# Recurrent core of a hybrid decoder step: the sample tile's heads stacked two to a quad slot, one on each half of the partitions

## The reference, cut to what matters

```
def step(S, inp):
    r_t, k_t, v_t, kk_t, a_t, w_t = inp
    sa = jnp.einsum('bhij,bhj->bhi', S, -kk_t)
    S = S * w_t[:, :, None, :] + sa[..., None] * (kk_t * a_t)[:, :, None, :] + v_t[..., None] * k_t[:, :, None, :]
    return S, jnp.einsum('bhij,bhj->bhi', S, r_t)
S_T, y = lax.scan(step, wkv0.astype(jnp.float32), seq)
```

## Time and profile before

| what | us |
| --- | --- |
| timed runs, median (lowest to highest) | 2816.4 (2814.28 to 2817.8) |
| profiled execution, its own time | 2817.6 |
| its span, first to last instruction | 2815.9 |
| recurrent core, first turn to last state product | 966.6 to about 1380 |
| quads 0 and 1 (samples, first half of the heads) | 966.56 to 1029.15 |
| quads 6 and 7 (samples, second half, with eight prompt steps) | 1159.23 to 1232.02 |

### The profile page before, as it was taken

One profiled execution on the slowest core, in us unless ns is written; L12 is line 12 of the kernel. 1 busy time (PEld: TensorE's weight loads), 2 busy tenths in 40 slices (PEclk: granted clock), 3 DMA queues, 4 the chain that ended last, 5 costly groups with the idle time before them and its releaser, 6 DMA issues. The chain is left out here.

```text
span 2815.9 us, 34250 instructions
## 1 busy us (share of the span) xinstructions
PE 2583.5 (92%) x13680; PEld 1442.8 (51%) x13680; DVE 748.5 (27%) x1366; ACT 454.5 (16%) x899; POOL 177.2 (6%) x180
## 2 busy tenths in 40 slices
PE   7999998999988888988699797799999999999996
PEld 4656765555554766766544555444333433443332
DVE  1045702122113635545420211211111121111112
ACT  2121023333323312112100212000000000000001
POOL 0000003011010122223000000000000000000000
PEclk9999999999998869779799986899999999999998
DMA  5512353777762101000244215399999999999996
GB/s 176 165 60 90 120 163 110 273 247 272 266 222 76 64 8 24 1 16 14 106 155 149 91 60 190 135 420 407 392 406 404 391 405 405 403 393 389 405 420 243
DMA packets 198788, 615.14 MB, mean 218 GB/s; under 512 B 37566, under 2 KB 113149, under 8 KB 147501
## 3 DMA queue, kind: packets, MB, share of 16 engines
q1 hardware_dynamic: 186045, 572.78, 53.2%
q0 software_dynamic: 10272, 35.96, 3.9%
q10 hardware_dynamic: 2320, 4.23, 0.4%
HBM read 600.66 MB, written 15.01 MB: 219 GB/s over the span
## 5 line engine op out<-in xcount | busy, mean ns | idle before, releaser
L360 PE MATMUL bank<-ht,w 128*128 128x320 f32 (+1 forms) x1888 | 566.3, 441 | 3.7 <-PEq L237 2.6
L2481 PE MATMUL bank<-wexp,fr 128*64 128x512 f32 x2048 | 445.7, 593 | 1.5 <-DVE fr L2392 1.5
L360 PEld LDWEIGHTS bank<-ht,w 128*128 128x128 f32 (+1 forms) x1888 | 342.0, 192 | 140.5 <-issue 29.5
L2481 PEld LDWEIGHTS bank<-wexp,fr 128*64 128x64 f32 x2048 | 149.1, 137 | 282.8 <-issue 281.5
L2534 PE MATMUL bank<-wexp,ut 128*64 128x512 f32 x1024 | 223.5, 594 | 11.4 <-ACT ut L2444 11.0
L2399 DVE TENSOR_TENSOR x<-x,bank 128x512 f32<-128x512 f32 x160 | 110.0, 688 | 376.4 <-PE bank L2493 368.4
L2534 PEld LDWEIGHTS bank<-wexp,ut 128*64 128x64 f32 x1024 | 72.0, 137 | 152.5 <-issue 136.5
L2461 PE MATMUL bank<-oh,hn 128*128 128x256 f32 x512 | 129.4, 396 | 8.2 <-DVE oh L2385 6.8
L1082 PE MATMUL bank<-work,fr 128*128 128x512 f32 x256 | 116.4, 614 | 6.7 <-DMA work<-in_w_out 5.7
L2493 PE MATMUL bank<-ys,sg 128*128 128x512 f32 x256 | 115.8, 606 | 2.0 <-ACT sg L2434 2.0
L2461 PEld LDWEIGHTS bank<-oh,hn 128*128 128x128 f32 x512 | 93.1, 192 | 46.3 <-issue 27.3
(11 more groups left out here) (403 smaller groups left out, 2686.7 us busy)
## 6 DMA issues: line engine op xcount, KB each, us to landing
wexp<-in_w_e SPq DMA_DIRECT2D x384, 1024.0 KB, 12.2
w<-in_w_in SPq DMA_DIRECT2D x29, 2048.0 KB, 8.6
work<-in_cache_k SPq DMA_DIRECT2D x64, 512.0 KB, 5.4
x<-in_cache_v POOLq DMA_DIRECT2D x64, 512.0 KB, 5.7
work<-in_w_out SPq DMA_DIRECT2D x4, 2048.0 KB, 19.1
work<-in_w_out SPq DMA_DIRECT2D x2, 4096.0 KB, 13.2
work<-in_w_cq SPq DMA_DIRECT2D x1, 4096.0 KB, 13.8
ckk<-in_cache_mem_k SPq DMA_DIRECT2D x8, 512.0 KB, 7.7
```

Source lines behind the costliest of these rows:

```text
L360: ins = e.matmul(self.bank[self.bank_no[n]][:width, 0:TOK], self.w[:, c % 2, k, j:j + width], self.ht[:, k, :], start=(k == 0), stop=(k == ...
L2481: ins = e.matmul(half(bank[u // 4], a_), xg[buf][:, kk, P * h + SLOTS * a_:P * h + SLOTS * a_ + SLOTS], w[:, u % RING, a_, DE * k:DE * k + ...
```

## The change

For the sample tile the two quads of a group become one quad of eight heads. What was a head's slot now holds a pair of heads: the 64 tokens of one on partitions 0 to 63, those of the other on partitions 64 to 127. Each matmul of a slot becomes two, one with its operands and its output on the lower half, one on the upper (`each`, and the loops over `r`). The instructions of DVE, ACT and POOL then take 128 partitions where they took 64, once where they came twice. The eight turns of a quad become 32 matmuls of 64x64 by a 64-wide part of the identity. POOL's spread is written as eight instructions of 512 elements in place of twice four of 1024. A spot of a merged quad holds two of the 16 places, so that group 3 has one prompt step at every spot where it had one at every second. Maps and additions go through their banks in two turns (b = 0, 1), and the second waits for the copies of the first. The masks `ab8`, `lo8` and `em8` are repeated on the upper half. Prompt quads keep their instructions; only the numbers that they wait for are counted anew (`f0`).

```diff
-    em8 = p[:, None] // CS == np.arange(8)[None, :]
+    em8 = p[:, None] % SS // CS == np.arange(8)[None, :]
...
+    tms, bxs, vxs = view(wf, 10240, 4, 4, HD), view(xf, 0, 4, 8, HD), view(xf, 2048, 4, 8, HD)
...
     def quads():
+        k = 0
         for gi, (hg, ti) in enumerate(GROUPS):
             t0, m = TILES[ti]
-            for q in range(2):
-                yield 2 * gi + q, gi, hg, ti, t0, m, q, 4 * hg + 2 * q
+            for q in range(1 if ti == 2 else 2):
+                yield k, 2 * gi + q, gi, hg, ti, t0, m, q, 4 * hg + 2 * q
+                k += 1
+
+    def taken(buf, f, ti, i):
+        return buf[:, f // 2 % 2, 2 * (f % 2) + i, :, :]
+
+    def places(ti, q, spot):
+        return (2 * spot, 2 * spot + 1) if ti == 2 else (8 * q + spot,)
...
-            for k, gi, hg, ti, t0, m, q, hp in quads():
-                em = cw("em16" if ti < 2 else "em8")[:m, 0:E].unsqueeze(2)
+            for k, f0, gi, hg, ti, t0, m, q, hp in quads():
                 g.wait_ge(tm_read, 2 * k + 2)
                 if k:
-                    g.wait_ge(add_made, k)
+                    g.wait_ge(add_made, f0)
+                if ti == 2:
+                    em = cw("em8").unsqueeze(2).to_broadcast([P, 8, HD])
+                    for dst, col in ((bxs, 1), (vxs, 3)):
+                        for v_ in range(4):
+                            ins = g.tensor_tensor(dst[:, v_, :, :], tms[:, v_, col, :].unsqueeze(1).to_broadcast([P, 8, HD]), em, ALU.mult)
+                            if v_ % 2:
+                                ins.then_inc(bv_spread, 1)
+                    send(gi, range(16))
+                    continue
+                em = cw("em16").unsqueeze(2).to_broadcast([P, E, P])
                 for dst, col in ((bx, 1), (vx, 3)):
                     for p_ in range(2):
-                        g.tensor_tensor(dst[:m, p_, 0:E, :], tm[:m, p_, col, :].unsqueeze(1).to_broadcast([m, E, P]),
-                                        em.to_broadcast([m, E, P]), ALU.mult).then_inc(bv_spread, 1)
+                        g.tensor_tensor(dst[:, p_, 0:E, :], tm[:, p_, col, :].unsqueeze(1).to_broadcast([P, E, P]), em, ALU.mult).then_inc(bv_spread, 1)
                 send(gi, range(8 * q, 8 * q + 8))
...
+                if ti == 2:
+                    a.activation(xx[:, :, 0:HD], tms[:, :, 0, :], ACT.Copy).then_inc(x_begun, 1)
+                else:
+                    a.activation(xx[:, :, 0:HD], tm[:, :, 0, :].rearrange("t a (p j) -> t a p j", p=2), ACT.Copy).then_inc(x_begun, 1)
+                for place in places(ti, q, 0):
+                    chain(gi, place)
                 a.wait_ge(akv_made, k + 1)
-                a.activation(xx[:m, :, HD:P], bank[0][:m, 0:4 * HD].rearrange("t (h j) -> t h j", h=4), ACT.Copy).then_inc(x_begun, 1)
+                a.activation(xx[:, :, HD:P], bank[0][:, 0:4 * HD].rearrange("t (h j) -> t h j", h=4), ACT.Copy).then_inc(x_begun, 1)
...
+                for i in range(2 if ti == 2 else 0):
+                    v.wait_ge(ab_made, 6 * k + 2 * i + 2)
+                    v.tensor_tensor((ab, ak)[i][:, :, :, 0:m], bank[2 + 2 * i][:, :].rearrange("s (h a t) -> s h a t", h=4, a=2),
+                                    two.unsqueeze(1).to_broadcast([P, 4, 2, m]), ALU.mult).then_inc(ab_read, 2)
+                if ti == 2:
+                    v.wait_ge(ab_made, 6 * k + 6)
+                    v.tensor_tensor(a1[:, :, 0:m], bank[6][:, 0:4 * m].rearrange("s (h t) -> s h t", h=4),
+                                    low.unsqueeze(1).to_broadcast([P, 4, m]), ALU.mult).then_inc(ab_read, 2)
...
+                nf = 2 if ti == 2 else 1
+                for f in range(f0, f0 + nf):
+                    v.wait_ge(add_made, f + 1)
+                    for i in range(2):
+                        ins = v.tensor_copy(taken(nns, f, ti, i), bank[ADDB[i]][:, :].rearrange("p (c j) -> p c j", c=8))
+                    ins.then_inc(add_read, 1)
...
                     for i, src in enumerate((ar[:, 0], t1, t2, vv)):
-                        ins = e.transpose(bank[p_][:m, i * P:(i + 1) * P], src[:, hp + p_, tok], ident)
+                        if ti < 2:
+                            ins = e.transpose(bank[b][:, i * P:(i + 1) * P], src[:, hp + b, tok], ident)
+                        else:
+                            for p_ in (2 * b, 2 * b + 1):
+                                for r in (0, 1):
+                                    c = HD * (4 * (p_ % 2) + i)
+                                    ins = e.matmul(half(bank[b][:, c:c + HD], r), half(src[:, hp + p_, tok], r), half(ident, r)[:, HD * r:HD * r + HD],
...
+                def each(out, lhs, rhs):
+                    if ti < 2:
+                        return e.matmul(out, lhs, rhs, start=True, stop=True)
+                    e.matmul(half(out, 0), half(lhs, 0), half(rhs, 0), start=True, stop=True)
+                    return e.matmul(half(out, 1), half(lhs, 1), half(rhs, 1), start=True, stop=True)
...
                     for h in range(4):
-                        ins = e.matmul(bank[it % 2][:m, h * P:(h + 1) * P], up(h), xx[:m, h, :], start=True, stop=True)
+                        ins = each(bank[it % 2][:, h * P:(h + 1) * P], up(h), xx[:, h, :])
                     ins.then_inc(xm_made, 1)
                     if it < nit - 1:
                         for h in range(4):
-                            ins = e.matmul(bank[SQB[it][0]][:m, h * m:(h + 1) * m], lo(h), up(h), start=True, stop=True)
...
+                    for b in range(2):
+                        if b:
+                            e.wait_ge(map_read, f0 + 1)
+                        for p_ in (2 * b, 2 * b + 1):
+                            ins = each(bank[MAPB[p_ % 2]][:, :], xx[:, p_, 0:HD], bxs[:, p_, :, :])
+                        ins.then_inc(map_made, 1)
+                        if b:
+                            e.wait_ge(add_read, f0 + 1)
+                        else:
+                            for place in places(ti, q, 5):
+                                chain(gi, place)
+                            e.wait_ge(w_spread, 4 * k + 4)
+                        for p_ in (2 * b, 2 * b + 1):
+                            for i in range(2):
+                                for r in (0, 1):
+                                    ins = e.matmul(half(bank[ADDB[p_ % 2]][:, :], r), half(tms[:, p_, 1 + i, :], r),
+                                                   half((wx, vxs)[i][:, p_, :, :], r), start=(i == 0), stop=(i == 1))
+                        ins.then_inc(add_made, 1)
+                for place in places(ti, q, 6):
+                    chain(gi, place)
...
+                            else:
+                                out = bank[QYB][:, (4 * (i > 0) + h) * m:(4 * (i > 0) + h + 1) * m]
+                                for r in (0, 1):
+                                    ins = e.matmul(half(out, r), half(lhs, r), half(rhs[:, h, 1, 0:m], r), start=(i < 2), stop=(i != 1))
```

More of the change, by code:

```diff
@@ L858, in _ @@
[L858 to L863, removed]
+                for place in places(ti, q, 4) + places(ti, q, 5):
+                    chain(gi, place)
+                for f in range(f0, f0 + (2 if ti == 2 else 1)):
+                    a.wait_ge(map_made, f + 1)
+                    for i in range(2):
+                        ins = a.activation(taken(mts, f, ti, i), bank[MAPB[i]][:, :].rearrange("p (c j) -> p c j", c=8), ACT.Copy)
+                    ins.then_inc(map_read, 1)
@@ L1011, in _ @@
+                    if ti == 2:
+                        ins.then_inc(ab_made, 2)
+                if k:
+                    e.wait_ge(qy_read, 2 * f0)
+                e.wait_ge(tm_read, 2 * k + 2)
+                for h in range(4):
+                    if ti < 2:
+                        ins = e.matmul(bank[(6, 1)[h % 2]][:, (h // 2) * m:(h // 2 + 1) * m], half(ar[:, 0, hp + h // 2, tok], h),
+                                       half(t4[:, hp + h // 2, tok], h), start=True, stop=True)
                         if h >= 2:
@@ L1021, in _ @@
-                chain(gi, 8 * q)
-                vh = lambda h: tm[:m, h // 2, 3, HD * (h % 2):HD * (h % 2) + HD]
+                    else:
+                        for r in (0, 1):
+                            ins = e.matmul(half(bank[6][:, m * h:m * (h + 1)], r), half(ar[:, 0, hp + h, tok], r), half(t4[:, hp + h, tok], r),
+                                           start=True, stop=True)
+                if ti == 2:
+                    ins.then_inc(ab_made, 2)
+                for place in places(ti, q, 0):
+                    chain(gi, place)
@@ L1024, in _ @@
                 for h in range(4):
-                    ins = e.matmul(bank[0][:m, h * HD:(h + 1) * HD], ak[:m, h, 0, 0:m], vh(h), start=True, stop=True)
+                    ins = each(bank[0][:, h * HD:(h + 1) * HD], ak[:, h, 0, 0:m], vh(h))
                 ins.then_inc(akv_made, 1)
@@ new lines, in _ @@
+                for place in places(ti, q, 6):
+                    chain(gi, place)
```

(11 more changed lines are left out.)

136 lines of the change are left out of this document (69 added, 67 removed).

## The result

The changed kernel took 2742.2 us (median of five runs, 2728.4 to 2745.8) beside 2814.3 us of the kernel before in the same rounds: a ratio of 0.973, 95% interval 0.972 to 0.975. The forecast was 2747 us, in a range from 2739 to 2772. The median lies inside, but the ratio puts the kernel at 0.9731 x 2814.3 = 2738.6 us, just under the low end.

The account below looks back on a forecast made before the run. Sample quads were taken as bound by TensorE's matmuls, with short waits between. Group 0 (-32.7), group 3 (-35.4) and a prompt quad (-2.1) sum to -70.2, so 2817.6 us becomes 2747, range 2739 to 2772.

Parts of the forecast that it names:

- waits of group 3: Merged quad of group 3: TensorE's waits for hand-over, spread, read-out, export and slowed DVE steps, 5.4 us in sum.
- 2 us either way: Later stages: a shifted core lets the clock fall elsewhere, a small term of 2 us up or down.
- base of the sum: Whole kernel: the gains are subtracted from the profiled execution's 2817.6 us.
- Which clock the merged quads get: Merged quads: both halves at work give 2.4 GHz, in group 0 from the end of the first turns on.
- second case: Merged quads stay at 1.2 GHz: 2792 us, or 2770 with one of them at 2.4 GHz; chance 0.14.
- pairs' price: Matmuls paired on two halves overlap in one PSUM bank: a pair costs what one costs alone.
- third case: Pairs don't overlap, since both write one bank, and run at 1.2 GHz: 2880 us, slower; chance 0.04.
- Group 0: Merged quad of group 0: 23.2 + 1.5 + 5.2 = 29.9 us for 62.59, a gain of 32.7.
- price by elements: POOL's spread in a merged quad: eight instructions take 7.45 us again, hidden before the maps; by instruction 14.9.
- Group 3: Merged quad of group 3: 23.2 + 8.8 + 5.4 = 37.4 us for 72.79, a gain of 35.4.
- The prompt quads: Prompt quad after group 0 starts with the clock up: -2.1 us, bounds 0 and -3; other prompt quads 0.
- forecast case: 2.4 GHz in both merged quads: 2747 us, its own range 2739 to 2758; chance 0.78.

Follow-up runs that it names:

- second pair of profiles: The changed kernel and the kernel before, each profiled once more with no edit; the spans differ by 2816.2 - 2742.7 = 73.5 us.
- four corners: Changed kernel with odd pairs' tokens on the other half and additions that need no spread first; timed 2735.0 us, 0.971 of the kernel before.

## Why the prediction was right, and where it was not

The mechanism stood; three sizes failed, and with them the low end of the range: the waits of group 3 (5.4 us put in, 3.25 measured), the "2 us either way" for the clock elsewhere (between two profiles of one program up to 6.1 us in the core and 8.1 ahead of it), and the base of the sum (2817.6 us from one execution, where the timed median was 2814.3).

*Which clock the merged quads get*: right, and now shown for these quads. A partner on the other half alone brings 2.4 GHz to the old quads (48.40 us for 68.69), its removal takes it from the new ones (47.37 for 29.42), and the same matmuls half after half lose it (51.90). The second case (1.2 GHz) is out by the rows of both merged quads. Two corners at work are not enough: the old maps and additions overlap on two corners as well, both on the lower rows (0.854 us a product, where two maps alone on one corner took 3.41 us at that clock with half of the matmuls left out, 1169.01 to 1172.42), and stayed at 1.2 GHz with 9.30 of 9.30 us busy. Nor do both halves decide everywhere: the last chunk steps use both, and with dead products between them stayed at 1.2 GHz with 14.87 of 14.87 us busy; why is open. The Trainium skill (TensorE: Matmul & The Clock Gate, Part 1: The HAM clock gate) has activity release the clock. If that means plain busy time, the trace does not agree: 0.50 with 27.77 of 30.70 us busy.

*The pairs' price*: right, and the third case is out. A pair of 128 columns takes 0.22 us in one bank; in the kernel before, with the clock still up, one product alone took (973.20 - 972.30) / 4 = 0.225:

```profile
972.30 1.05 PE L1036 MATMUL bank<-work 64*64 64x128 f32 x8 [0.56 <-ACT work L848]
...
973.20 0.99 PE L1040 MATMUL bank<-work 64*64 64x64 f32 x8
```

Maps and additions gain by the clock alone, since they overlapped before too: 0.43 us a product for 0.854, as put in.

*Group 0*: 29.15 and 29.42 us for 29.9. TensorE was busy for 25.0 us (24.7 put in) and waited 4.1 (5.2 put in). POOL's eight spreads took 8.04 us, near the price by elements (7.45) and far from the one by instruction (14.9), and ended before the maps.

*Group 3*: the size was off, 34.45 for 37.4. The term that failed is the sum of its waits: 5.4 put in, 3.25 measured. DVE's step instructions did take longer while POOL spread (1.24 and 1.15 us for 0.42), but of the delay 0.33 reached TensorE where I let 1.5; the export's wait was 0.98 for 1.6, the first hand-over 0.58 for 0.75; spread and read-out were 0.87 and 0.49 for 1.0 and 0.5. The other 0.8 is TensorE's own time.

*The prompt quads*: -2.1 in all was put in, for the first one alone. The second pair of profiles gives -2.2, the first -10.6. That the second agrees is luck: the two quads behind merged ones gained 1.8 and 1.6 us, and the others lost 1.2.

*The sum*: in the second pair -33.9 in group 0, -34.2 in group 3, -2.2 in the prompt quads and -1.4 in the last quad with its tail; ahead of the core -3.3, behind it +1.5. That is -73.5, for -70.2 forecast. In group 3 two errors offset one another: the new quad was put 2.9 us too high, and the old one, 68.69 in this pair, was subtracted at 72.79.

*The range*: the ratio's 2738.6 lies 0.4 us under its low end. One step that failed is "2 us either way" for the clock falling elsewhere. Two profiles of one program differ by 6.1 us in the core (changed) and 4.6 (before), and the way to the core by up to 8.1. Some 7 us beside the 8 us of the forecast case's own range, taken as independent, make 10.6 and a low end near 2736. The other is the base: the sum starts from one execution of 2817.6 us, where the timed median of the kernel before was 2814.3. From that, -70.2 gives 2744, and the same 8 us a low end of 2736. The direction, the mechanism and the two large terms stood.

## What to carry to other kernels

Where a matmul fills a quarter of the array, look for a partner for each free corner before looking at waits: here pairs brought 34 us a group, more than half of it in group 3 by the clock, and four corners another 5 to 8. Before subtracting from one profile, take a second one: here a group that changes its clock within itself moved by 4.1 us, and the way to the core by up to 8.1. Dead work that is to hold the clock is best tried with the first gap filled too: once the clock had fallen here, the dead work did not bring it back.

## What the hardware did that was not expected

- TensorE overlapped matmuls on different halves even when all four of one half stand before the four of the other in the program: 35.70 us for 29.42, where a wait that really parts them made 51.90. The first upper product started ahead of the fourth lower one, so the starts did not keep the program's order.
- 64x64 matmuls on four corners, outputs in two banks, took 0.87 us for four of 512 columns (two records each, 0.43 apart), the price of one.
- In the last chunk steps the clock stayed at 1.2 GHz with TensorE busy for all of 14.87 us, and with the gap ahead of them filled at 2.4, with 15.78 of 17.48 busy.
